# Expert layers of a diffusion trunk: GpSimd makes the pair sums and picks the dense tiles' experts head by head beside the queries, and 14 expert rows are taken ahead of the first weights

## The reference, cut to what matters

```
q = (xt @ w_q).reshape(n, 8, 2, 128)                 # 8 heads, 2 halves
s = einsum('thcd,hcnd->thcn', q, keys)               # scores against 128 keys a half: 16 "codes"
sv, si = top_k(s, 16)                                # 16 best keys of each code
cand = sv[:, :, 0, :, None] + sv[:, :, 1, None, :]   # sums of pairs
best, bi = top_k(cand, 16)                           # 16 best pairs of each head
i1 = take(si[:, :, 0], bi // 16); i2 = take(si[:, :, 1], bi % 16)
eidx = i1 * 128 + i2                                 # 8 x 16 = 128 experts of 16384 per token
gate = softmax(best)
act = gelu(einsum('td,ted->te', x, u_tab[eidx])) * gate
out = einsum('te,ted->td', act, v_tab[eidx])
```

## Time and profile before

| | |
|---|---|
| median of 3 runs | 4333.82 us (4330.99 to 4334.0) |
| profiled execution, its own time | 4334.56 us |
| its span, first to last instruction | 4332.5 us |
| busy: PE, DVE, POOL, ACT | 90%, 71%, 44%, 16% |
| granted TensorE clock, mean | 0.953 |
| read and written in HBM | 1116.99 MB, 48.37 MB |

### The profile page before, as it was taken

One profiled execution on the slowest core, in us unless ns is written; L12 is line 12 of the kernel. 1 busy time (PEld: TensorE's weight loads), 2 busy tenths in 40 slices (PEclk: granted clock), 3 DMA queues, 4 the chain that ended last, 5 costly groups with the idle time before them and its releaser, 6 DMA issues. The chain is left out here.

```text
span 4332.5 us, 46101 instructions
## 1 busy us (share of the span) xinstructions
PE 3902.8 (90%) x16342; PEld 2318.5 (54%) x16342; DVE 3092.6 (71%) x6176; ACT 688.1 (16%) x1432; POOL 1912.9 (44%) x1654
## 2 busy tenths in 40 slices
PE   8986899998899999899979997999888899899897
PEld 3643656775444444444347875577744444454442
DVE  6747635897877777778763146589788777777777
ACT  4122410162000000000013122103600000000000
POOL 0002200075677777766600000003777677777673
PEclk9997899999999999999989999999999999999999
DMA  4213741268999999999922105014899999999996
GB/s 185 82 46 117 270 155 43 75 180 290 375 420 420 420 419 420 418 420 414 418 109 67 59 20 127 23 56 124 268 362 375 420 420 419 420 420 419 414 419 266
DMA packets 375714, 1169.30 MB, mean 270 GB/s; under 512 B 35833, under 2 KB 120281, under 8 KB 364042
## 3 DMA queue, kind: packets, MB, share of 16 engines
q0 software_dynamic: 184960, 679.58, 38.8%
q1 hardware_dynamic: 107856, 445.02, 27.1%
q10 hardware_dynamic: 82684, 41.95, 3.4%
HBM read 1116.99 MB, written 48.37 MB: 269 GB/s over the span
## 5 line engine op out<-in xcount | busy, mean ns | idle before, releaser
L605 PE MATMUL banks<-h_dense_T,blocks 128*128 128x320 f32 x4096 | 1139.2, 433 | 0.0
L424 POOL DMA_INDIRECT expert_rows<-in_pk_u_dram,expert x640 | 830.3, 1297 | 384.4 <-DVE own_dots L890 202.4
L653 PE MATMUL banks<-blocks,picked_T 128*128 128x512 f32 x2048 | 999.7, 633 | 0.0
L605 PEld LDWEIGHTS banks<-h_dense_T,blocks 128*128 128x128 f32 x4096 | 778.4, 190 | 385.8 <-issue 98.4
L915 DVE SCALAR_TENSOR_TENSOR acc<-expert_rows,expert_weight,acc 128x1024 f32<-128x1024 f32 x628 | 793.9, 1283 | 249.2 <-DMA expert_rows<-in_pk_v_dram,expert 244.2
L424 POOL DMA_INDIRECT expert_rows<-in_pk_v_dram,expert x640 | 807.5, 1262 | 335.1 <-DVE acc L915 170.9
L890 DVE CUSTOM_DVE_ANT_0 expert_rows<-expert_rows,h_rows 128x1024 f32<-128x1024 f32 x640 | 774.2, 1225 | 240.2 <-DMA expert_rows<-in_pk_u_dram,expert 236.2
L653 PEld LDWEIGHTS banks<-blocks,picked_T 128*128 128x128 f32 x2048 | 389.3, 201 | 625.9 <-issue 625.9
L644 PE MATMUL banks<-blocks,picked_T 128*64 128x512 f32 x1024 | 298.1, 659 | 226.7 <-DVE picked_T L876 226.1
L448 ACT ACTIVATE dense_act<-banks 128x320 f32<-128x320 f32 x246 | 107.5, 437 | 2153.4 <-PE banks L605 2153.4
L412 POOL TENSOR_SCALAR expert_rows<-iota,picked_T 128x128 f32<-128x128 f32 x320 | 210.2, 675 | 442.2 <-ACT picked_T L454 394.4
(11 more groups left out here) (522 smaller groups left out, 3961.6 us busy)
## 6 DMA issues: line engine op xcount, KB each, us to landing
blocks<-in_pk_u_turned_dram SPq DMA_DIRECT2D x256, 512.0 KB, 6.5
blocks<-in_pk_v_dram SPq DMA_DIRECT2D x256, 512.0 KB, 6.5
ada_block<-in_ada_rest_dram SPq DMA_DIRECT2D x32, 1280.0 KB, 7.1
gates_dram<-shared ACTq DMA_DIRECT2D x40, 1024.0 KB, 5.5
shared<-gates_dram SPq DMA_DIRECT2D x32, 1280.0 KB, 10.5
blocks<-in_pk_w_q_dram SPq DMA_DIRECT2D x32, 512.0 KB, 3.5
expert_rows<-in_pk_u_dram,expert POOLq DMA_INDIRECT x640, 12.8
expert_rows<-in_pk_v_dram,expert POOLq DMA_INDIRECT x640, 13.4
```

The lines of the kernel that those rows point to most:

```text
L424: pool.indirect_dma_start(out=rows[:, r % RING, :], out_offset=None, in_=table, in_offset=bass.IndirectOffsetOnAxis(ap=idx[:, at_:at_ + 1] ...
L605: mm = pe.matmul(dense_dots(c), u[:, k * P:(k + 1) * P], HT[:, k, 0:DENSE], start=(k == 0), stop=(k == KD - 1))
L653: mm = pe.matmul(ps[:, at_:at_ + HALF], wt[:, c % WEIGHED, z * P:(z + 1) * P], v[:, half_ * HALF:(half_ + 1) * HALF], start=(c == 0), stop ...
```

## The change

On the dense tiles, the work that DVE did after the queries is now done head by head during them. POOL makes the sums of pairs of heads 0 to 6 (`pairs_dense`; DVE makes those of head 7). DVE searches them, works out the two ranks of each best pair at once and counts `searched`. POOL then picks the two halves of the expert's number (`pick_dense`), with a comparison, a product and a sum by halving over 3 x 16 x 16 elements a half. The softmax of the three tiles is made in one piece (`gates_dense`). PE's early dots fall from 16 to 7 chunks, 9 chunks lie in the gaps of the spread, and 9 after it. The rows' buffers get other slots, so that rows 0 and 1 don't touch the hots and the others follow as the spread frees slots; POOL's gathers no longer wait for the whole spread. DVE takes 14 rows ahead of the first weights, and the other 626 over the same chunks as before.

```diff
+SLOT_OF_ROW = (8, 9, 0, 4, 1, 5, 2, 6, 3, 7)
-GAPS = (7, 14, 21, 28, 35)
-EXTRA = len(GAPS)
+GAPS = (3, 7, 11, 15, 19, 23, 27, 31, 35)
+EXTRA = 5
-EARLY = (0, 9, 13, 16)
-MIDDLE = EARLY[-1] + EXTRA
+EARLY = (0, 5, 6, 7)
+EXPS_AT = 2
+MIDDLE = EARLY[-1] + len(GAPS)
+ROWS_BEFORE = 14
...
+def hots_through(r):
+    return DENSE - HOTS + 8 * (r // 2)
...
-    return min(ROWS, ROWS * passes_by(c) // passes_by(ROWS_DONE))
+    return min(ROWS, ROWS_BEFORE + (ROWS - ROWS_BEFORE) * passes_by(c) // passes_by(ROWS_DONE))
...
+            def pairs_dense(h):
+                pool.wait_ge(score_used, 2 * h + 2)
+                if h >= 2:
+                    pool.wait_ge(searched, h - 1)
+                for at_, a, many, few in BLOCKS_OF_PAIRS:
...
+                    line.count(ins)
+                line.settle()
+                pool.sem_inc(pairs_made, 1)
+
+            def pick_dense(h):
+                pool.wait_ge(searched, h + 1)
+                line.count(pool.tensor_copy(top[:, 0:ND, 2 * h:2 * h + 2], where[:, 0:ND, 2 * h:2 * h + 2]))
+                line.then(pool.tensor_copy(ranks_f, ranks_of(h)))
+                wide = [P, ND, TOPK, TOPK]
+                for a in range(2):
+                    line.then(pool.tensor_tensor(
+                        one_of_dense, iota17[:, 1 - a:1 - a + TOPK].unsqueeze(1).unsqueeze(1).to_broadcast(wide),
+                        ranks_f[:, a].unsqueeze(3).to_broadcast(wide), ALU.subtract))
+                    line.then(pool.tensor_scalar(one_of_dense, one_of_dense, 0.0, None, ALU.is_equal))
+                    line.then(pool.tensor_tensor(
+                        one_of_dense, one_of_dense,
+                        top[:, 0:ND, 2 * h + a, :].unsqueeze(2).to_broadcast(wide), ALU.mult))
+                    half_ = TOPK // 2
+                    while half_ > 1:
+                        line.then(pool.tensor_tensor(
+                            one_of_dense[:, :, :, 0:half_], one_of_dense[:, :, :, 0:half_],
+                            one_of_dense[:, :, :, half_:2 * half_], ALU.add))
+                        half_ //= 2
...
+                pool.sem_inc(picks_done, 1)
+
+            for h in range(HEADS):
+                if h < HEADS - 1:
+                    pairs_dense(h)
+                if h:
+                    pick_dense(h - 1)
+            pick_dense(HEADS - 1)
...
-            pool.wait_ge(spread, DENSE)
...
+                    if r % FREED == 0 and 0 < r < RING:
+                        pool.wait_ge(spread, hots_through(r))
                     if r % FREED == 0 and r + FREED > RING:
                         pool.wait_ge(row_used, r + FREED - RING)
...
-                if z:
-                    exponentials(z)
                 for c in range(EARLY[z], EARLY[z + 1]):
-                    if c == 6:
-                        exponentials(0)
+                    if c == EXPS_AT:
+                        exponentials_dense()
                     gelu(c)
                 columns(z)
...
             def columns(z):
-                pe.wait_ge(cols_set, z + 1)
+                pe.wait_ge(cols_set, 1)
+                pe.wait_ge(picks_done, HEADS)
...
             for c in range(CODES):
                 by_code(c)
-                if c % 2 == 1:
-                    by_head_dense(c // 2)
-            for z in range(ND):
-                for _ in experts_of(z, best_of[:, z], at_of[:, z]):
-                    pass
+                if c % 2 == 0 and c:
+                    by_head_dense(c // 2 - 1)
+            by_head_dense(HEADS - 1)
+            gates_dense()
...
             for _ in range(BEFORE):
                 next(last)
+            for _ in range(ROWS_BEFORE):
+                next(taken)
```

More of the change, by code:

```diff
@@ new lines, in by_head_dense, with gates_dense @@
+                line.then(dve.tensor_tensor(at_h[:, 1], at_h[:, 1], block_of_dense,
+                                            ALU.logical_shift_right))
+                dve.sem_inc(searched, 1)
+            def gates_dense():
+                shape = [P, ND, HEADS, TOPK]
+                e = picked[:, 0:ND, 2, :].rearrange("p z (h k) -> p z h k", h=HEADS)
+                dve.tensor_tensor(e, best_of[:], best_of[:, :, :, 0:1].to_broadcast(shape),
+                                  ALU.subtract).then_inc(exp_in, 1)
+                dve.wait_ge(exp_out, 1)
+                line.then(dve.tensor_reduce(e_sum[:], e, AX.X, ALU.add))
+                line.then(dve.reciprocal(e_sum[:], e_sum[:]))
+                line.then(dve.tensor_tensor(e, e, e_sum[:, :, :].unsqueeze(3).to_broadcast(shape),
+                                            ALU.mult))
+                dve.sem_inc(cols_set, 1)
+                for q in range(WAYS):
+                    line.count(dve.tensor_copy(
+                        own_gate[q * OWN:(q + 1) * OWN, :],
+                        picked[P - OWN:P, ND - 1, 2, q * OWN_STEPS:(q + 1) * OWN_STEPS]))
+                dve.wait_ge(picks_done, HEADS)
+                for q in range(WAYS):
+                    some = slice(q * OWN_STEPS, (q + 1) * OWN_STEPS)
+                    line.count(dve.scalar_tensor_tensor(
+                        out=idx[q * OWN:(q + 1) * OWN, 0:OWN_STEPS],
+                        in0=picked[P - OWN:P, ND - 1, 0, some], scalar=float(P),
+                        in1=picked[P - OWN:P, ND - 1, 1, some], op0=ALU.mult, op1=ALU.add))
+                line.settle()
+                dve.sem_inc(idx_ready, 1)
@@ L821, in experts_of @@
                     dve.sem_inc(g_free, 1)
[L822 to L838, removed]
+                at_ = UNIT_AT[i - ND + 1]
+                dve.scalar_tensor_tensor(
+                    out=idx[:, at_:at_ + SLOTS], in0=picked[:, i, 0, :], scalar=float(P),
+                    in1=picked[:, i, 1, :], op0=ALU.mult, op1=ALU.add).then_inc(idx_ready, 1)
                 yield
-                line.then(dve.reciprocal(e_sum[:], e_sum[:]))
+                dve.wait_ge(exp_out, i - ND + 2)
+                line.then(dve.tensor_reduce(e_sum[:, 0], e_of(i), AX.X, ALU.add))
+                yield
+                line.then(dve.reciprocal(e_sum[:, 0], e_sum[:, 0]))
                 yield
                 line.then(dve.tensor_tensor(
[L843 to L851, removed]
+                    e_of(i), e_of(i), e_sum[:, 0].unsqueeze(2).to_broadcast([P, HEADS, TOPK]), ALU.mult))
                 yield
```

73 lines of the change are left out of this document (57 added, 16 removed).

## The result

The changed kernel took 4396.36 us (median of 4 runs, 4391.35 to 4401.25) against 4333.91 for the kernel before (4 runs): ratio 1.0148, 95% interval 1.0135 to 1.016. It is slower by 1.5%; the prediction said 4310 (4298 to 4325), faster. The profiled execution took 4396.64 us, with a span of 4394.8.

A forecast was written before the change was run, and what follows sets the result against it. The prediction took the main loop as bound by the bytes DMA must bring, with idle DMA time before it as what could be saved. A gain of 12 us a stage, 24 in all, off 4333.8 gave 4310 us (4298 to 4325).

The forecast's parts named there:

- the ledger: First stage, 826 to 1180: DMA idle time of 95.4 us falls to 84.2, a gain of 11.2 us.
- POOL's new work: POOL during the queries: a pick takes 14.5 us, with bounds of 12.8 and 20, plus 0.9 for a head's sums.
- the rival of the slow picks: POOL's picks at 20 us end at 890, a loss of 12 us a stage, 4358 us; chance 0.18.
- the 18.2 from which I had called the gain gone: POOL's picks: above 18.2 us a pick, the gain of 11.2 us a stage is gone.
- When the picks are done, and PE: End of queries and spread: picks done at 867, spread from 880.5 to 995, nine more chunks of dots to 1034.
- DVE and the gates: Before the main loop: first weights stay at about 1030; DVE's 14 rows end near 1016 to 1020, covered by the gates.
- it moves nothing: Around the spread's end: 14 rows crowd out the gates' last writes, first weights 10 us later, 4325 to 4342; chance 0.15.
- The sum: Both stages: row count gives 14 to 17.7 us, idle DMA time 11.2; taken as 12 a stage, 24 in all.
- Counting rows (17.7): Main loop: fourteen fewer rows at 1.26 us each save 17.7 us a stage, if DMA can bring them earlier.
- Contention: POOL and DVE slow each other in the queries: picks an eighth longer, gain 6 us a stage, 4322; no chance given.

The follow-up runs named there:

- e1: The changed kernel with the enlarged exp_sum moved behind all other buffers, so the ring starts at byte 78848 again: 4341.72 us, ratio 1.0026 to the kernel before.
- e2: The kernel before with a spare of 64 bytes a partition ahead of the ring, which starts at byte 78912: 4382.79 us, ratio 1.0121.
- e3: The kernel before with 224 spare bytes at the right end, so weight blocks and gates start at multiples of 256 bytes: 4335.36 us, ratio 1.0016.
- e5: e1 with DVE picking the experts of heads 6 and 7 and POOL those of heads 0 to 5: 4316.01 us, ratio 0.995.
- e4: e1 with POOL's gathers waiting for the whole spread and no row taken ahead of the first weights: 4342.32 us, ratio 1.0027.
- e6: e4 with 14 rows again taken ahead of the first weights: 4324.62 us, ratio 0.9981.
- e7: e6 and e5 together, gathers held behind the spread and the two last picks on DVE: 4302.20 us, ratio 0.9918.
- e8: The kernel before with a spare of 128 bytes a partition ahead of the ring, which starts at byte 78976: 4387.50 us, ratio 1.0116.

## Why the prediction was wrong

- **The main loop's rate.** The step that failed most is the ledger's own ground: that a row is "1.26 us at 420 GB/s", a rate taken over to the changed kernel, which has 410. No rival asked what else the diff moves. The larger `exp_sum` moved the ring and what lies behind it by 64 bytes, which by e1 is 1.22 points of the 1.48 (53 us), and by e2 1.21 on a kernel with nothing else changed. The Trainium skill (DMA: Bandwidth & Descriptors, section "How a descriptor splits into AXI transactions") says that a descriptor is read in transactions of up to 256 bytes that must start at a multiple of 256. Worked out from that rule, as an estimate, 4096 bytes that start elsewhere take 17 transactions in place of 16, 6% more. The rule is told of reading, and the ring is what the gathers write, so I carry it over. The runs agree in where it bites (64 and 128 bytes cost the same, 256 nothing), but not in the size, as a row's packet takes 2.5% longer (159.2 to 163.1 ns). They also don't agree for the blocks, of the same width on SP's queue, which take 159.2 ns at 224 bytes past a multiple (before) and at a multiple (e3). Why stays open.
- **POOL's new work.** The step failed by one term: the comparison was sized from a scalar instruction with a product or a sum, 1046 ns for 1024 elements, and took 2140 for 768. The row of a comparison stood in the earlier trace rows too: L412, 675 ns for 128 elements, which I read as a long start and left to the rival of the slow picks. The two sizes together make an estimated 2.3 ns an element and 0.4 us of start, though L412 compares with a number for each partition and L455 with zero. Two of L455 make the 2.7 us that a pick is over 14.5; the casts (0.27 each, 0.95 foreseen for both) and the other instructions cancel. At 17.2 us the picks end 9 us later than foreseen, still under the 18.2 from which I had called the gain gone. By e5's rate (25.7 us of time for 13.4 us of the spread in each stage) this is an estimated 17 us of the 32 that lie between 4310 and e1.
- **When the picks are done, and PE.** With that, the places came as worked out: POOL's chain behind code 13 (its sums of head 6 start at 155.8 from the stage's start, foreseen at 155), the spread 111.3 us long (114.5 foreseen) with hardly a wait, nine chunks of 4.32 behind it. From the spread's start at 221, 111.3 and nine chunks make 371, where e4 has the first sums. DVE's share of the queries went up to 107.48 us (105.67), and PE stayed at 126.00.
- **DVE and the gates.** The sentence "with more traffic I put the weights at about 1030, unchanged" was the third error. The last write of the gates takes 36.5 us to land among 24 gathers, 11 of them issued before it, and 19.5 among ten; the first sums came 21 us later. Holding the gathers back gives 17 us (e6 against e1). This is the mechanism of the rival "it moves nothing", to which I gave 0.15; no row in my text spoke against it, as the earlier trace rows already had DMA at 0.93 there. That e1's 4341.7 also lies in its 4325 to 4342 is in part luck, since half of what e1 is over 4310 is the picks', which this rival doesn't hold.
- **The three together.** 53 for the ring, 17 for the picks and 17 for the gates' write, on 4310, make 4397, and 4396 was measured. Each term is good to a few us, so that the sum meets so closely is luck too.
- **The sum.** The ledger of idle time was the right measure. Over the first 600 us of the first stage the kernel before moves 227 GB/s, e1 225, e6 231 and e7 241. Each GB/s more is 0.6 MB, or 1.4 us at 420: by that e1 would end 3 us later, e6 5.7 earlier and e7 20 earlier, and they ended 0.4, 6.5 and 19.7 us earlier. In the second stage the rates are 230, 226, 232 and 240, so 5.7 later, 2.9 and 14.3 earlier, against 6.5 later, 4.7 and 17.9 earlier. It holds to within 4 us. Counting rows (17.7) says nothing while the ring stands still afterwards.
- **Contention.** POOL slows DVE in a few small instructions. DVE's four pair sums of the last head in the changed kernel, while POOL picks:

```profile
846.96 1.95 DVE L825 TENSOR_TENSOR sums<-top_value 128x48 f32<-128x48 f32 x4
```

and in e7_all, where POOL has finished:

```profile
847.16 0.57 DVE L824 TENSOR_TENSOR sums<-top_value 128x48 f32<-128x48 f32 x4
```

It isn't only instructions with two inputs: the shift of 48 elements on DVE's L842, with one, takes 186 to 789 ns in the changed kernel, median 396, against a median of 190 in e7. POOL's product took 1.80 to 1.85 us with DVE busy or idle, and its difference 1.49 to 1.69; the pick of head 6 beside DVE's last search took 17.4 us and that of head 7, with DVE nearly idle, 16.9. So the picks lost some tenths by it.

## What to carry to other kernels

When a diff resizes or adds any buffer, work out where the buffers behind it now start, above all those that gathers write to: here a start off a multiple of 256 bytes cost 1.2%, and the busy share of DMA didn't show it; the GB/s and the time of a packet did. Work taken ahead of a DMA-bound loop is worth only the DMA idle time that it removes, counted until the loop runs full; and transfers issued just ahead of or behind a write that others wait for delay that write. Price each operation from a row of the same operation, and not only of the same opcode (L2063 and L455 are both `TENSOR_SCALAR`), or bound it by the dearest of its kind.

## What the runs showed of the hardware that was not expected

- Software gathers of 4096 bytes a partition into a ring that starts 64 or 128 bytes past a multiple of 256 bytes: 410 GB/s at a DMA share of 1.03 in place of 420, a packet of 4096 bytes 163.1 to 163.6 ns in place of 159.2, the blocks' packets beside them too (e2, e8). The blocks on SP's queue, themselves 224 bytes past a multiple, lose nothing that shows (e3).
- POOL's scalar `is_equal` takes 2.14 us for 768 elements a partition (changed kernel), against 1.81 for a product of two inputs of that size; DVE compares two tensors of that size in 0.96 (e7).
- A write of 1 MB on ACT's queue took 6.22 us to be issued and 36.5 to land while POOL issued 24 gathers of 0.53 MB, against 0.4 and 5.8 (median of five writes) around the end of the spread in the kernel before, whose last one took 19.5.
